# Linear attention in 64-row and 64-column groups of the array, two heads at a time

## The chip, the cores and the metric

One core of a Trainium2 chip runs the whole program as one launch. The metric is the device time of that launch in microseconds (us). TensorE (PE in the rows) multiplies, VectorE (DVE) and ScalarE (ACT) read its results from PSUM, GpSimd (POOL) works in SBUF, and SyncE issues the weight stream.

## What is computed

A trunk of two layers, 512 tokens of width 1024. Each layer mixes tokens by three groups of heads (linear attention, sparse attention, latent attention), then runs an MLP. Only the linear attention is touched, four heads with keys of 64 and values of 128, in 8 chunks of 64 tokens:

```python
q_dec = qc * jnp.exp(b)
k_inv = kc * jnp.exp(-b)
scores = jnp.where(causal, jnp.einsum('bnhcd,bnhsd->bnhcs', q_dec, k_inv), 0.0)
o_intra = jnp.einsum('bnhcs,bnhsv->bnhcv', scores, vc)
k_end = kc * jnp.exp(b_end - b)
state_inc = jnp.einsum('bnhcd,bnhcv->bnhdv', k_end, vc)
...
def step(state, inp):
    dec, inc = inp
    return dec[..., None] * state + inc, state
...
o = o_intra + jnp.einsum('bnhcd,bnhdv->bnhcv', q_dec, s_prev)
```

## The kernel before

Everything is written out by hand: one instruction stream for each engine, semaphores between them, and a table (`USES`) that gives each PSUM tile one of eight banks in a fixed order. A tile may be written once the tile before it in its bank has been read (`vacant`); `freed` says that a tile has been read, `filled` that it has been written.

A layer runs: 24 units of input projection (TensorE, matmuls of 128x128 weights on 512 columns), then the attention stage, then the output projection and the MLP.

The attention stage goes over 32 steps j (`N_ATT`), each one query block of one softmax head; the first 16 are the latent attention. For each step TensorE computes logits three steps ahead (`logits`, `LEAD`), VectorE masks them (`mask_max`), ScalarE takes exponentials, VectorE normalises (`normalise`), TensorE transposes (`turn`), ScalarE copies (`turned`), and TensorE weighs values for two steps at a time (`weigh_pair`). The linear attention is woven between these:

- `gla_scores(h)`, at the start and at j = 0, 2, 4: k_inv times q_dec, one head at a time, 128 tokens by 128 tokens. The queries lie in `gqp`, a tile of 128 rows for each head of which 64 are zero, so that the product over 128 rows holds one head only. `masked_scores` (VectorE) copies the two 64x64 diagonal blocks to `sct`, whose other blocks are zero.
- the increments, into banks `inc00` to `inc11`: `ke` holds the keys twice, each time with one of every two chunks zero. One bank holds four chunks of two heads, the heads in the column halves of the array.
- VectorE adds them up to the states `st` (lines 1474 and 1476), 7 steps for each pair of heads, each waiting for the one before.
- `gla_out(h)`, at j = 1, 3, 5, 7, one head at a time, banks 0 and 7 in turn: masked scores times values, plus states times queries.
- for each head then: square (ScalarE), `stat` (TensorE, a sum over rows by a matrix of ones), `factor` (ScalarE, logarithm and exponential), `mix` (VectorE, which also frees the bank of `gla_out`), `mix_high`, `mix_low`.

GpSimd clears `gqp`, `sct` and `ke` in each layer (lines 420, 429, 434).

A matmul in fp32 stands in the trace as two weight loads and two matmuls; "record" below means one such matmul.

Of the kernel before, what the change touches and what calls it, by code (L numbers as in the profile page):

```python
# [20 lines left out]
P = 128  # L21
# [84 lines left out]
TURNING = ["gs0"] + [f"lg{j}" for j in range(LEAD)]  # L106
for _j in range(N_MLA):
    TURNING += [f"lg{_j + LEAD}"] if _j + LEAD < N_MLA else []
    TURNING += [f"gs{SCORE_SLOT[_j]}"] if _j in SCORE_SLOT else []
    TURNING += [f"gst{STAT_SLOT[_j]}"] if _j in STAT_SLOT else []  # L110

# [10 lines left out]
def part_of(j):  # L122
# [18 lines left out]
    + [(name, (2, 3, 6)[i % 3]) for i, name in enumerate(TURNING[:1 + LEAD])]  # L141
    + [("inc00", 4), ("inc01", 5), ("inc10", 6), ("inc11", 7)]
    + [(name, (2, 3, 6)[i % 3]) for i, name in enumerate(TURNING) if i > LEAD]
# [58 lines left out]
def build_trunk(nc, x_in, stream, params, consts, out):  # L202
    with ExitStack() as ctx:
# [45 lines left out]
        sct, _ = place("sct", [P, 2, TB, P], at=a0 + 8192)  # L249
# [69 lines left out]
        zeroed = S("zeroed", 4)  # L319
# [77 lines left out]
        def _(pool):  # L397
# [18 lines left out]
            with pool.Fori(0, DEPTH) as l:  # L416

                pool.wait_ge(*x_ready.at(l, -1))
                alone(pool)
                pool.memset(gqp[:], 0.0).then_inc(zeroed.sem, 1)  # L420
                pool.wait_ge(*lo_ready.at(l, POOL_LOW[0] + AHEAD - 1))
                for u in POOL_LOW:
# [3 lines left out]
                    if u == 11:  # L426
                        pool.wait_ge(*rel_used.at(l, 3 * IDX_H - 1))
                        alone(pool)
                        pool.memset(sct[:], 0.0).then_inc(zeroed.sem, 1)
                    if u == 19:  # L430
                        pool.wait_ge(*B.filled(l, "mv1"))
                        alone(pool)
                    if u in (19, 21):
                        pool.memset(ke[:, (u - 19) // 2], 0.0).then_inc(zeroed.sem, 1)
# [22 lines left out]
        def _(pe):  # L457
# [58 lines left out]
            with pe.Fori(0, DEPTH) as l:  # L516
# [156 lines left out]
                def gla_scores(h):  # L673
                    pe.wait_ge(*B.vacant(l, f"gs{h}"))
                    for tb in range(TB):
                        tk = slice(tb * P, (tb + 1) * P)
                        m = pe.matmul(B[f"gs{h}"][:, tk], kinv[:, h // 2, tk], gqp[:, h, tk], start=True, stop=True)
                    m.then_inc(*B.on_fill(f"gs{h}"))

                def gla_out(h):  # L680
                    name = f"go{h}"
                    pe.wait_ge(*B.vacant(l, name))
                    pe.wait_ge(*B.freed(l, f"gs{h}"))
                    if h == 0:
                        pe.wait_ge(*B.freed(l, "inc11"))
                    for tb in range(TB):
                        pe.matmul(B[name][:, tb * P:(tb + 1) * P], gvt[:, tb, h * GLA_DV:(h + 1) * GLA_DV],
                                  sct[:, h % 2, tb], start=True, stop=False)
                        for c in (2 * tb, 2 * tb + 1):
                            if c == 0:  # L690
                                continue
                            m = pe.matmul(B[name][:, c * CHUNK:(c + 1) * CHUNK], st[:, c, h // 2],  # L692
                                          gqp[:, h, c * CHUNK:(c + 1) * CHUNK], start=False,
                                          stop=(c % 2 == 1))
                    m.then_inc(*B.on_fill(name))
# [67 lines left out]
                for j in range(LEAD):  # L763
                    logits(j)
# [100 lines left out]
        def _(act):  # L865
# [27 lines left out]
            with act.Fori(0, DEPTH) as l:  # L893
# [194 lines left out]
                for j in range(N_ATT):  # L1088
# [6 lines left out]
                    if j in STAT_SLOT:  # L1095
                        factor(f"gst{STAT_SLOT[j]}", GLA_DV)
# [582 lines left out]
```

## Time and profile before

| | us |
|---|---|
| median of 3 runs | 1317.99 |
| lowest and highest | 1312.17, 1323.12 |
| profiled execution | 1319.28 |
| its span | 1317.6 |
| TensorE busy | 1261.7 (96%) |
| VectorE busy | 773.5 (59%) |
| ScalarE busy | 538.5 (41%) |
| GpSimd busy | 247.3 (19%) |

The mean granted TensorE clock is 0.988 of full speed. The attention stage begins at 188.2 us in layer 0 and at 835.3 us in layer 1. "Idle before" in the rows is the time in which the engine stood still ahead of the instruction, with what ended it.

### The profile page before, as it was taken

The page shows a single profiled execution, that of the slowest core. Times are in us where ns is not written, and L with a number is a line of the kernel's source. Part 1 is how long each engine was busy: PE and PEld are TensorE (multiplying, and loading weights), DVE is VectorE, ACT ScalarE, POOL GpSimd, SP SyncE. Part 2 cuts the span into 40 slices and gives each one's busy share as a digit, 9 for nine tenths or more (in the row PEclk, how much of TensorE's full clock was granted, in tenths as well). Part 3 has the DMA queues.
Part 4 walks back from the last instruction along what each step waited for, and adds up shares of the span by engine and source line. Part 5 has one row for each costly group of instructions (what it writes and reads, how often), then busy time and mean ns, then how long its engine had stood idle before and what let it go on. Part 6 is the DMA issues. An engine that isn't in the chain of part 4 may idle for free.

```text
span 1317.6 us, 19119 instructions
## 1 busy us (share of the span) xinstructions
PE 1261.7 (96%) x5912; PEld 987.6 (75%) x5912; DVE 773.5 (59%) x1236; ACT 538.5 (41%) x863; POOL 247.3 (19%) x157
## 2 busy tenths in 40 slices
PE   4999999899999999999999999988999999999997
PEld 3856776478888888888877568765788888888886
DVE  4579866624464554544766888564445544445458
ACT  4474435734422313223436643375443132232343
POOL 4022340002021020110531323200111201102016
PEclk9999999889999999999999999999999999999999
DMA  5211220013222222222222112100232223223233
GB/s 199 99 49 64 64 97 1 2 48 122 97 98 91 101 96 96 96 96 96 96 98 81 59 54 81 65 2 1 91 113 96 96 95 100 92 96 108 89 104 127
DMA packets 31023, 110.46 MB, mean 84 GB/s; under 512 B 3568, under 2 KB 3568, under 8 KB 30960
## 3 DMA queue, kind: packets, MB, share of 16 engines
q1 hardware_dynamic: 29088, 103.82, 23.2%
q0 software_dynamic: 576, 3.76, 0.8%
q10 hardware_dynamic: 1296, 2.12, 0.5%
q8 instruction: 30, 0.49, 0.2%
q14 instruction: 33, 0.27, 0.1%
HBM read 107.59 MB, written 2.10 MB: 83 GB/s over the span
## 4 chain that ended last, share of the span: by engine, by line
PE 89%; DVE 3%; ACT 3%; issue 3%; POOL 1%; DMA 1%; DVEq 0%; ACTq 0%; SPq 0%; POOLq 0%
PE bank L821 18%; PE bank L819 18%; PE bank L820 18%; PE bank L476 6%; PE bank L477 6%; PE bank L478 6%; PE bank L510 2%; PE bank L499 2%; PE bank L498 2%; PE bank L497 2%; PE bank L708 1%; PE bank L735 1%; PE bank L720 1%; PE bank L692 1%; POOL lnb L409 1%
## 5 line engine op out<-in xcount | busy, mean ns | idle before, releaser
L874 ACT ACTIVATE wh<-raw 128x1024 fp32r<-128x1024 f32 x194 | 204.8, 1056 | 394.1 <-PE bank L821 239.0
L1153 DVE TENSOR_TENSOR wl<-raw,wh 128x1024 fp32r<-128x1024 f32 x158 | 246.9, 1563 | 98.5 <-ACT wh L874 91.0
L819 PE MATMUL bank<-hh,wl 128*128 128x512 f32 x512 | 200.0, 391 | 0.0
L819 PE MATMUL bank<-xmh,wl 128*128 128x512 f32 x512 | 199.3, 389 | 0.0
L821 PE MATMUL bank<-hl,wh 128*128 128x512 f32 x512 | 199.2, 389 | 0.0
L821 PE MATMUL bank<-xml,wh 128*128 128x512 f32 x512 | 199.2, 389 | 0.0
L820 PE MATMUL bank<-xmh,wh 128*128 128x512 f32 x512 | 199.2, 389 | 0.0
L820 PE MATMUL bank<-hh,wh 128*128 128x512 f32 x512 | 199.2, 389 | 0.0
L444 POOL TENSOR_TENSOR x<-x,rsb 128x512 f32<-128x512 f32 x64 | 84.5, 1320 | 580.3 <-DVE rsb L1531 580.3
L476 PE MATMUL bank<-xgh,wl 128*128 128x512 f32 x368 | 152.4, 414 | 22.8 <-DVE xgl L1162 17.3
L1520 DVE TENSOR_TENSOR sqb<-tf 128x512 f32<-128x512 f32 x64 | 44.3, 692 | 181.4 <-ACT hh L1124 181.4
L477 PE MATMUL bank<-xgh,wh 128*128 128x512 f32 x368 | 145.2, 394 | 0.0
L478 PE MATMUL bank<-xgl,wh 128*128 128x512 f32 x368 | 144.9, 394 | 0.0
L424 POOL TENSOR_TENSOR wl<-raw,wh 128x1024 fp32r<-128x1024 f32 x36 | 86.5, 2403 | 236.7 <-ACT wh L874 236.7
L1122 ACT ACTIVATE tf<-bank 128x512 f32<-128x512 f32 x64 | 38.3, 598 | 204.5 <-PE bank L821 204.5
L1531 DVE TENSOR_TENSOR rsb<-bank,rb 128x512 f32<-128x512 f32 x64 | 44.3, 691 | 116.8 <-PE bank L821 113.2
L820 PEld LDWEIGHTS bank<-hh,wh 128*128 128x128 f32 x512 | 96.1, 188 | 20.6 <-issue 0.5
L819 PEld LDWEIGHTS bank<-hh,wl 128*128 128x128 f32 x512 | 96.1, 188 | 20.3 <-issue 0.5
L476 PEld LDWEIGHTS bank<-xgh,wl 128*128 128x128 f32 x368 | 69.8, 190 | 55.2 <-DVE xgl L1162 21.4
L819 PEld LDWEIGHTS bank<-xmh,wl 128*128 128x128 f32 x512 | 96.1, 188 | 20.1 <-DVE xml L1162 0.4
L820 PEld LDWEIGHTS bank<-xmh,wh 128*128 128x128 f32 x512 | 96.1, 188 | 20.0
L821 PEld LDWEIGHTS bank<-xml,wh 128*128 128x128 f32 x512 | 96.1, 188 | 20.0
(187 smaller groups left out, 1757.7 us busy)
## 6 DMA issues: line engine op xcount, KB each, us to landing
raw<-in_stream SPq DMA_DIRECT2D x194, 512.0 KB, 3.2
x<-in_x ACTq DMA_DIRECT2D x8, 256.0 KB, 12.8
out_y<-x SPq DMA_DIRECT2D x8, 256.0 KB, 4.3
par<-in_params POOLq DMA_DIRECT2D x2, 916.0 KB, 4.8
con<-in_consts POOLq DMA_DIRECT2D x1, 944.5 KB, 9.1
par<-in_params POOLq DMA_DIRECT2D x1, 896.0 KB, 11.3
par<-in_params ACTq DMA_DIRECT2D x1, 20.0 KB, 2.6
```

The costliest lines, as they stand in the source:

```text
L424: pool.tensor_tensor(wl[:, u % 2], raw[:, u % 2], wh[:, u % 2], ALU.subtract)\
L444: pool.tensor_tensor(x[:, d], x[:, d], rsb[:, d % 2], ALU.add).then_inc(x_ready.sem, 1)
L476: pe.matmul(bank[:], wk_l, act_h[:, k], start=(n == 0), stop=False)
L477: pe.matmul(bank[:], wk_h, act_h[:, k], start=False, stop=False)
L478: m = pe.matmul(bank[:], wk_h, act_l[:, k], start=False, stop=last)
L819: pe.matmul(B.t[s][:], wl[:, s, n_block(k)], src_h[:, k], start=(k == 0), stop=False)
L820: pe.matmul(B.t[s][:], wh[:, s, n_block(k)], src_h[:, k], start=False, stop=False)
L821: m = pe.matmul(B.t[s][:], wh[:, s, n_block(k)], src_l[:, k], start=False, stop=(k == KB - 1))
L874: act.activation(wh[:, s], raw[:, s], ACT.Copy).then_inc(hi_ready.sem, 1)
L1153: vec.tensor_tensor(wl[:, s], raw[:, s], wh[:, s], ALU.subtract).then_inc(lo_ready.sem, 1)
L1520: vec.tensor_tensor(sqb[:, s], tf[:, s], tf[:, s], ALU.mult).then_inc(hid_ready.sem, 1)
L1531: vec.tensor_tensor(rsb[:, s], B.t[s][:], rb[:], ALU.mult).then_inc(dn_freed[s].sem, 1)
```

## The change

- Scores: 64x64 matmuls, unpadded. The rows of the array are split by head, the columns by the parity of the chunk. Both heads of a pair come from one call, `gla_scores(pr)`, each in its own bank.
- `gqp` holds both heads of a pair in one tile; `sct` holds only the diagonal blocks; `masked_scores(pr)` makes one copy of 128 rows for each head. `ke` is a plain copy.
- Increments: the rows are split by the parity of the chunk, the columns by head; banks hold even and odd chunks.
- `gla_out(pr)`: two heads into two banks, rows split in halves. Matmuls of one bank always come from one half of the rows; halfway the halves change over, and TensorE waits there for its own last matmul (`rows_done`).
- The outputs come at j = 1 and 5 (pairs), the second pair's scores at j = 2, the sums of squares at j = 3 and 7, two at a time.
- The increments are now ahead of the second and third logits, and on VectorE the second and third `mask_max` stand between the states of the first and of the second pair.
- GpSimd clears nothing.

```diff
-SCORE_SLOT = {2 * h - 2: h for h in range(1, GLA_H)}
-OUT_SLOT = {2 * h + 1: h for h in range(GLA_H)}
-STAT_SLOT = {2 * h + 3: h for h in range(GLA_H)}
+SCORE_SLOT = {2: 1}
+OUT_SLOT = {1: 0, 5: 1}
+STAT_SLOT = {3: 0, 7: 1}
...
-    + [("inc00", 4), ("inc01", 5), ("inc10", 6), ("inc11", 7)]
+    + [("inc00", 4), ("inc01", 5), ("inc10", 0), ("inc11", 1)]
...
+                def gla_scores(pr):
+                    for hp in range(2):
+                        pe.wait_ge(*B.vacant(l, f"gs{2 * pr + hp}"))
+                    alone(pe)
+                    for c in range(NCHUNK):
+                        r = slice(CHUNK * (c % 2), CHUNK * (c % 2) + CHUNK)
+                        keys = slice(c * CHUNK, (c + 1) * CHUNK)
+                        for hp in range(2):
+                            k = slice(GLA_DK * hp, GLA_DK * hp + GLA_DK)
+                            m = pe.matmul(B[f"gs{2 * pr + hp}"][r, c // 2 * CHUNK:(c // 2 + 1) * CHUNK],
+                                          kinv[k, pr, keys], gqp[k, pr, keys], start=True, stop=True)
...
+                    for c in range(0, NCHUNK, 2):
+                        within(0, c, c == 0, False)
+                        within(1, c + 1, c == 0, False)
+                        across(0, c + 1)
+                        if c > 0:
+                            across(1, c)
+                            across(0, c)
+                        mine = across(1, c + 1)
+                        if c == NCHUNK - 2:
+                            mine.then_inc(rows_done.sem, 1)
+                            pe.wait_ge(*rows_done.at(l, pr))
+                    for c in range(0, NCHUNK, 2):
+                        m0 = within(0, c + 1, False, c == NCHUNK - 2)
+                        m1 = within(1, c, False, c == NCHUNK - 2)
...
+                    for c in range(NCHUNK - 1):
+                        name = f"inc{pr}{c % 2}"
+                        r = slice(CHUNK * (c % 2), CHUNK * (c % 2) + CHUNK)
+                        for hp in range(2):
+                            h = 2 * pr + hp
+                            m = pe.matmul(B[name][hp * 64:(hp + 1) * 64, c // 2 * P:(c // 2 + 1) * P],
+                                          ke[r, 0, c // 2, h * GLA_DK:(h + 1) * GLA_DK],
+                                          gvt[r, c // 2, h * GLA_DV:(h + 1) * GLA_DV], start=True, stop=True)
...
+                masked_scores(0)
+                mask_max(0)
+                states(0)
+                for j in range(1, LEAD):
+                    mask_max(j)
+                states(1)
```

`within` is masked scores times values of one chunk (64 rows, 128 columns of the array, 64 columns moving), `across` is state times queries of one chunk, of the same shape.

TensorE at the start of the attention stage, before. The names are tiles; 128x128 after them is the output's shape, and x4 is the number of matmuls in a row.

```order
L677 MATMUL bank<-gqp,kinv 128x128 x4
L701 REGISTER_ALU
L708 MATMUL bank<-kT,qT 128x128
L701 REGISTER_ALU
L708 MATMUL bank<-kT,qT 128x128
L701 REGISTER_ALU
L708 MATMUL bank<-kT,qT 128x256
L768 REGISTER_ALU x2
L777 MATMUL bank<-gvt,ke 64x128 x14
L773 REGISTER_ALU
L777 MATMUL bank<-gvt,ke 64x128 x14
L701 REGISTER_ALU
```

The same place in the changed kernel:

```order
L662 REGISTER_ALU x2
L669 MATMUL bank<-gqp,kinv 64x64 x16
L721 MATMUL bank<-kT,qT 128x128
L779 REGISTER_ALU x2
L790 MATMUL bank<-gvt,ke 64x128 x14
L783 REGISTER_ALU x2
L790 MATMUL bank<-gvt,ke 64x128 x14
L714 REGISTER_ALU
L721 MATMUL bank<-kT,qT 128x128
L714 REGISTER_ALU
L721 MATMUL bank<-kT,qT 128x256 x2
L730 REGISTER_ALU
```

Four padded score matmuls became 16 small ones for two heads; the second and third logits moved behind the increments, whose number stays 28.

VectorE between its mask of the logits and the states, before (ISA is the masking instruction, COPY the first state of a pair):

```order
L1442 REGISTER_ALU
L1447 ISA pb,nb<-bank,con 128x128
L1447 ISA nb 128x1
L1442 REGISTER_ALU
L1447 ISA pb_92,nb<-bank,con 128x256
L1447 ISA nb 128x1
L1471 REGISTER_ALU
L1474 COPY st<-bank 128x128
L1178 REGISTER_ALU
L1476 SCALAR_TENSOR_TENSOR st<-st,e_59,bank 128x128
```

And in the changed kernel, from the last state of the first pair on:

```order
L1486 REGISTER_ALU
L1481 SCALAR_TENSOR_TENSOR st<-st,e_59,bank 128x128
L1454 REGISTER_ALU
L1459 ISA pb,nb<-bank,con 128x128
L1459 ISA nb 128x1
L1454 REGISTER_ALU
L1459 ISA pb_92,nb<-bank,con 128x256
L1459 ISA nb 128x1
L1477 REGISTER_ALU
L1479 COPY st<-bank 128x128
```

The two masks stood ahead of all states and now stand between the two pairs'.

TensorE from the sum of squares of j = 3 to the outputs of j = 5, before:

```order
L510 MATMUL bank<-sqb,ones 128x512
L701 REGISTER_ALU
L708 MATMUL bank<-kT,qT 128x512
L674 REGISTER_ALU
L677 MATMUL bank<-gqp,kinv 128x128 x4
L717 REGISTER_ALU
L718 REGISTER_ALU
L720 MATMUL bank<-con,pb 128x128 x3
L701 REGISTER_ALU
L708 MATMUL bank<-kT,qT 128x128
L718 REGISTER_ALU
L720 MATMUL bank<-con,pb 128x128 x3
```

And in the changed kernel:

```order
L497 MATMUL bank<-sqb,ones 128x512
L496 REGISTER_ALU
L497 MATMUL bank<-sqb,ones 128x512
L714 REGISTER_ALU
L721 MATMUL bank<-kT,qT 128x512
L730 REGISTER_ALU
L731 REGISTER_ALU
L733 MATMUL bank<-con,pb 128x128 x3
L721 MATMUL bank<-kT,qT 128x128
L731 REGISTER_ALU
L733 MATMUL bank<-con,pb 128x128 x3
L676 REGISTER_ALU x2
```

Two sums of squares stand where one stood, and no scores are left between them and the next outputs (behind the last row in both).

## Rows read from the trace of the kernel before

**Rows 1.** Groups by line and shape, both layers: busy us, mean ns | idle before

```profile
L692 PE MATMUL bank<-gqp,st 128*128 128x64 f32 x112 | 16.6, 267 | 0.0
...
L687 PE MATMUL bank<-sct,gvt 128*128 128x128 f32 x64 | 14.9, 316 | 1.5 <-DVE tf L1420 1.5
...
L677 PE MATMUL bank<-gqp,kinv 128*128 128x128 f32 x64 | 8.6, 278 | 2.9 <-DVE st L1476 2.9
```

**Rows 2.** Timeline of TensorE, start of the attention stage, layer 0

```profile
188.23 1.05 PE L677 MATMUL bank<-gqp,kinv 128*128 128x128 f32 x8
189.12 0.61 PE L708 MATMUL bank<-kT,qT 96*128 96x128 f32 x4
...
191.07 3.28 PE L777 MATMUL bank<-gvt,ke 128*64 128x128 f32 x56
194.28 0.70 PE L708 MATMUL bank<-kT,qT 96*128 96x256 f32 x2
196.41 1.16 PE L677 MATMUL bank<-gqp,kinv 128*128 128x128 f32 x8 [1.43 <-DVE st L1476]
198.26 0.33 PE L720 MATMUL bank<-con,pb 128*128 128x128 f32 x1 [0.69 <-DVE pb L1454]
...
199.20 0.38 PE L687 MATMUL bank<-sct,gvt 128*128 128x128 f32 x2
...
201.60 0.86 PE L708 MATMUL bank<-kT,qT 96*128 96x384 f32 x2
```

**Rows 3.** Timeline of ScalarE and then VectorE, same stretch

```profile
189.51 1.26 ACT L1057 ACTIVATE gvt<-bank,rcol 128x512 f32<-128x512 f32 x2
...
192.20 0.29 DVE L1474 COPY st<-bank 128x128 f32<-128x128 f32 x1 [0.65 <-PE bank L777]
...
197.72 0.16 DVE L1453 RECIPROCAL rinv<-rsum 128x1 f32<-128x1 f32 x1
```

**Rows 4.** Timeline of TensorE, four matmuls of the indexer in four row groups

```profile
54.28 0.31 PEld L595 LDWEIGHTS bank<-ikr,iqT 32*128 32x128 f32 x8 [0.35 <-issue]
...
54.81 0.61 PE L595 MATMUL bank<-ikr,iqT 32*128 32x512 f32 x4
...
55.35 0.50 PE L476 MATMUL bank<-xgh,wl 128*128 128x512 f32 x1
```

**Rows 5.** Timeline of TensorE, sums of squares and the last head's outputs, layer 0

```profile
207.36 1.13 PE L510 MATMUL bank<-sqb,ones 128*128 128x512 f32 x2
208.32 1.02 PE L708 MATMUL bank<-kT,qT 96*128 96x512 f32 x2
...
217.60 0.49 PE L687 MATMUL bank<-sct,gvt 128*128 128x128 f32 x2 [0.77 <-DVE tf L1420]
```

**Rows 6.** Timeline of ScalarE and VectorE after the first sum of squares

```profile
208.60 0.69 ACT L926 ACTIVATE lnb<-bank,con 128x512 f32<-128x512 f32 x1 [3.25 <-PE bank L510]
209.32 0.63 ACT L930 ACTIVATE rsb<-lnb 128x512 f32<-128x512 f32 x1
...
209.57 0.69 DVE L1447 CUSTOM_DVE_ANT_0 pb<-bank,con 128x512 f32<-128x512 f32 x1 [2.73 <-PE bank L708]
...
210.18 0.74 DVE L1420 SCALAR_TENSOR_TENSOR tf<-bank,par,rsb 128x512 f32<-128x512 f32 x1
210.96 0.69 DVE L1427 TENSOR_TENSOR tf<-tf,gg 128x512 f32<-128x512 f32 x1
```

**Rows 7.** Timeline of TensorE behind the linear attention; then busy us of PE, PEld, DVE, ACT, POOL

```profile
230.91 0.49 PE L708 MATMUL bank<-dkn,dqn 64*128 64x128 f32 x4 [1.55 <-DVE nb L1447]
...
228.00:232.00 4.00, 2.45 (x14) 1.34 (x13) 3.75 (x11) 2.88 (x9) 0.00 (x0) 0.94 0.00 0
```

**Rows 8.** A stretch of layer 1, same columns, then PEclk; then TensorE there

```profile
845.00:847.00 2.00, 1.62 (x6) 1.08 (x7) 1.53 (x9) 0.91 (x4) 0.00 (x0) 0.72 0.00 0
...
845.38 0.33 PE L720 MATMUL bank<-con,pb 128*128 128x128 f32 x1 [0.71 <-DVE pb L1454]
...
856.12 1.12 PE L510 MATMUL bank<-sqb,ones 128*128 128x512 f32 x2
```

More of the change, by code:

```diff
@@ L671, in _ @@
                 pe.wait_ge(*B.freed(l, "gk1"))
[L673 to L695, printed above, removed]
@@ new lines, in gla_out, with within, across @@
+                def gla_out(pr):
+                    for hp in range(2):
+                        pe.wait_ge(*B.vacant(l, f"go{2 * pr + hp}"))
+                        pe.wait_ge(*B.freed(l, f"gs{2 * pr + hp}"))
+                    pe.wait_ge(*B.freed(l, f"inc{pr}0"))
+                    def within(hp, c, start, last):
+                        h, r = 2 * pr + hp, slice(CHUNK * (c % 2), CHUNK * (c % 2) + CHUNK)
+                        return pe.matmul(B[f"go{h}"][:, c * CHUNK:(c + 1) * CHUNK],
+                                         gvt[r, c // 2, h * GLA_DV:(h + 1) * GLA_DV], sct[r, hp, c // 2],
+                                         start=start, stop=last)
+                    def across(hp, c):
+                        h, k = 2 * pr + hp, slice(GLA_DK * hp, GLA_DK * hp + GLA_DK)
+                        return pe.matmul(B[f"go{h}"][:, c * CHUNK:(c + 1) * CHUNK], st[k, c, pr],
+                                         gqp[k, pr, c * CHUNK:(c + 1) * CHUNK], start=False, stop=False)
+                    for c in range(0, NCHUNK, 2):
[12 more added lines that the diff above has]
+                        m1 = within(1, c, False, c == NCHUNK - 2)
+                        if c == NCHUNK - 2:
+                            m0.then_inc(*B.on_fill(f"go{2 * pr}"))
+                            m1.then_inc(*B.on_fill(f"go{2 * pr + 1}"))
@@ L762, in _ @@
                 gla_scores(0)
-                for j in range(LEAD):
-                    logits(j)
+                logits(0)
                 for tb in range(TB):
@@ L1092, in _ @@
                     if j - 1 in OUT_SLOT:
-                        h = OUT_SLOT[j - 1]
-                        square(f"gst{h}", B[f"go{h}"][:], wait=B.filled(l, f"go{h}"))
+                        for h in range(2 * OUT_SLOT[j - 1], 2 * OUT_SLOT[j - 1] + 2):
+                            square(f"gst{h}", B[f"go{h}"][:], wait=B.filled(l, f"go{h}"))
                     if j in STAT_SLOT:
-                        factor(f"gst{STAT_SLOT[j]}", GLA_DV)
+                        for h in range(2 * STAT_SLOT[j], 2 * STAT_SLOT[j] + 2):
+                            factor(f"gst{h}", GLA_DV)
                     if j - 1 in STAT_SLOT:
-                        mix_high(STAT_SLOT[j - 1], STAT_SLOT[j - 1])
+                        for h in range(2 * STAT_SLOT[j - 1], 2 * STAT_SLOT[j - 1] + 2):
+                            mix_high(h, h)
                     if j % PAIR == LAG and j > PAIR:
@@ L1496, in _ @@
                     if j - 1 in STAT_SLOT:
-                        h = STAT_SLOT[j - 1]
-                        mix(h, f"gst{h}", f"go{h}", G_GLA + h, gate=h)
+                        for h in range(2 * STAT_SLOT[j - 1], 2 * STAT_SLOT[j - 1] + 2):
+                            mix(h, f"gst{h}", f"go{h}", G_GLA + h, gate=h)
                     if j - 2 in STAT_SLOT:
-                        mix_low(STAT_SLOT[j - 2])
+                        for h in range(2 * STAT_SLOT[j - 2], 2 * STAT_SLOT[j - 2] + 2):
+                            mix_low(h)
                     if j % PAIR == LAG + 3 and j > PAIR:
```

87 lines of the change are left out of this document (32 added, 55 removed).

## The prediction

> **What bounds the kernel now.** I read the groups by line first, to see how much work the change can touch at all. The scores are 64 records over both layers, the two lines of the outputs 112 and 64 [rows 1], the increments 56 in one layer [rows 2]. In a stream they follow each other at intervals much shorter than their own durations, so their cost has to be read as start to start. Then the timeline of the attention stage of layer 0 [rows 2]: eight score records go from 188.23 to 189.12, 0.111 us each; one head's outputs go from 199.20 to 201.60, 22 records, 0.109 us each, though 14 of the 22 move only 64 columns. A record of 64 columns costs as much as one of 128 here: the load of 128 weight columns sets the pace, 0.11 us. The 56 increment records take 191.07 to 194.28, 0.057 us each, since two halves of the columns run side by side, 0.115 us for a pair.
>
> So a layer spends on TensorE: scores 4 x 0.89 = 3.56 us, increments 3.2 us, outputs 4 x 2.4 = 9.6 us, 16.4 us together, 33 us in 1317.6 [rows 1, 2]. Nothing outside can move by much, and even a halving of all of this would be 1.3%.
>
> Which engine ends a wait decides how much of it shows. From 188 to 198.3 it is VectorE: TensorE waits 1.43 and 0.69 us, and the first transpose (198.26) follows the first normalisation (197.72), which follows the chain of states from 192.2 to 197.7 [rows 2, 3]. From 198.3 to about 225 TensorE hardly waits: 0.77 us ahead of the last head's outputs, for the mix that frees its bank [rows 5]. From about 226 on VectorE takes part again: TensorE waits 1.55 us for a mask ahead of 230.91, and VectorE is busy for 3.75 of the 4 us from 228 on [rows 7].
>
> **What a record costs in row groups.** The trace of before has this for the indexer, four matmuls in four groups of 32 rows [rows 4]. Eight weight loads end within 0.31 us, where one after another they would take 8 x 0.11 = 0.9. So loads into different row groups go side by side. The second four matmuls start at 54.81, 0.53 after the first, which is a load (0.10) and 0.43 of streaming 512 columns: their own loads were done meanwhile. And the next full matmul starts at 55.35, 0.11 after the last stream's end (54.81 + 0.43), and loads again for 0.11: each change between full array and groups costs about 0.2 us in and 0.2 us out.
>
> From this, for one pair of heads, with both row halves running side by side:
> - Outputs: 30 records in each half (22 ahead of the changeover, 8 behind), each paced by its load of 128 weight columns: 30 x 0.109 = 3.27. One entry 0.2, and at the changeover the array runs dry and loads anew. No row shows a wait of TensorE for itself; from below it is a load (0.11), from above the 0.69 us of a wait for another engine [rows 2]. I take 0.35, near the low end, since no other engine works in between. The exit falls together with the entry to the next weighing. Sum 3.8 us against 2 x 2.4 = 4.8. Gain 1.0, twice in a layer.
> - Scores: each quarter of the array gets 8 records of 64 weight columns and 64 moving, half the increments' 0.109 each, 8 x 0.055 = 0.45. With entry and exit 0.85 against 1.78. Gain 0.9 for each pair.
> - Increments: 16 records for the fuller quarters at 0.109, 1.75 us against 3.2. Gain 1.45.
>
> **What of it shows**, in layer 0:
>
> Start of the stage. The increments start when ScalarE has copied the values (189.51 + 1.26 = 190.8, [rows 3]), which nothing changes. The first pair's 28 records now take 8 x 0.109 + 0.1, and the state chain needs all of them where it needed 16 records before (0.92 us): it starts at 192.2 again. It is as long as it was, 14 steps, but with two masks in between, 0.2 and 0.4 us. So the first transpose is 0.6 us later, at about 198.85. What scores and increments save here becomes TensorE's idle time: it would be done at 194.2 and stand for 4.6 us. Cost +0.6.
>
> Outputs of both pairs: -2.0. The second pair's scores, at j = 2: -0.9.
>
> The second pair's outputs, at j = 5. They wait for the banks of both heads of the first pair, freed by two mixes on VectorE. Before, head 2 at j = 5 needed one mix only, and started right when it was done (210.18 + 0.74, [rows 6]). Now the two sums of squares take 2 x 0.96 us [rows 5], the factor of the second head another 1.3 us of ScalarE behind the first (0.69 + 0.63), and the second mix stands behind a whole first (0.74 + 0.69). Counted from TensorE's own order: sums of squares start about 207.1 and end 209.0; logits of 512 columns to 209.9; transposes and logits to 210.8. On the other side: these logits are read at 210.1 and masked to 210.75, first mix to 212.1, second mix frees the bank at 212.85. TensorE stands for 2.1 us. Before, it stood 0.77 us at j = 7, which goes. Cost +1.3.
>
> Sum to the last sum of squares: 0.6 - 2.0 - 0.9 + 1.3 = -1.0. Behind that VectorE decides [rows 7]. The same operations stand there in another order (the mix of head 3 comes earlier, together with that of head 2); their start comes about 0.5 us earlier as I count it, since two factors must now end before the second mix. I keep -0.5 of the -1.0.
>
> Off the path, at nothing: GpSimd's clears (GpSimd is 81% idle), one multiplication of 0.69 us for each pair on VectorE in the projection, where TensorE is fully busy, and two of four copies of `ke` on ScalarE, which waits for TensorE next to them. If their cover went, they could only shorten the time.
>
> Layer 1 has the same shape. Both: -1.0 us.
>
> **The clock.** The granted clock drops to its lower level (1.2 GHz, 0.5 of full) now and then in the attention stage. One place is telling: in layer 1 it is 0.72 on average from 845 to 847, right after TensorE had stood 0.71 us [rows 8]; in layer 0, after nearly the same waits, it stayed up. From its first transpose (845.38) to the first sum of squares (856.12) it takes 10.74 us, layer 0, at full clock, 198.26 to 207.36, 9.10 [rows 2, 5]. A drop there costs 1.64 us. The change gives TensorE a longer rest just there, 4.6 us, so I expect the drop in both layers: +1.6.
>
> The sum on the profiled execution: 1319.28 - 1.0 + 1.6 = 1319.9, and the median of the runs lies 1.3 below the profiled one: **1318.6, say 1319 us.** The three runs spread from 1312 to 1323, so 1% (13 us) is about what a measurement can tell.
>
> **Rivals.**
>
> *TensorE is all that counts.* If the waits I added (2 x 0.6 and 2 x 1.3) don't come, and the work behind moves up with it, then -2.9 in a layer remains of the window, and with a changeover near 0.1 us -3.4: 6 to 7 us, some 1311 without the extra drop of the clock. Against it speak two chains I can write down step by step. 0.15.
>
> *Weight loads aren't hidden in the small groups (slower).* If loads of the two halves go one after another, the outputs of a pair take 60 x 0.11 = 6.6 + 0.55 = 7.1 instead of 4.8: +2.3 twice in a layer, while the scores (64 columns a load, 32 x 0.055 = 1.8 + 0.4) lose 0.4 instead of gaining 0.9. A layer then comes to 4.6 + 0.4 + 1.9 (the two waits) = +6.9 at the most, some 14 us, 1333 with the clock's part. It decides from 0.14 us a record: at 30 x 0.14 + 0.55 the outputs of a pair cost 4.8, as now. The eight loads in 0.31 us speak against it [rows 4], but they are one burst and not a stream. A milder form: the halves run side by side, but in each half load and stream add up, 0.11 + 0.055 = 0.165 a record. Then a pair's outputs take 30 x 0.165 + 0.55 = 5.5, +0.7 twice, a pair's scores 8 x 0.11 + 0.4 = 1.3, -0.5, and with the two waits (+1.9) a layer comes to +2.8: 5.6 and the clock's 1.6 make 1325. 0.07 for both, 0.04 of it the milder.
> The Trainium skill's page "TensorE: Matmul & The Clock Gate" says, in Part 3 under "What overlaps and what doesn't", that a weight load overlaps matmuls in flight only where the row group differs, which is the milder form. This trace disagrees: four of the eight loads were done while matmuls of the same four row groups ran, since the second matmuls follow the first without one.
>
> *The clock (slower).* The rests of 4.6 and 2.1 us bring a second drop in each layer, at 1.6 each: 1319 + 3.3 = 1322, or with a longer first drop 1326. For it: the drop shown here followed a wait. Against: a later drop of the stage could as well go when the work in front of it moves. 0.16.
>
> *The main case*, the waits eat the gain: 0.62: 1319.
>
> **Range.** The unknown costs (changeover 0.1 to 0.7, four times: -1 to +1.4; a drop more or less: 1.6 each) give 1314 to 1324 for the main case. With the median's own scatter and the clock's case up to 1326 I give 1311 to 1327. Faster than 1305 would need more than all of TensorE's savings on the path: 0.03. Slower than 1331 needs the weight loads one after another (0.03) or several long drops of the clock (0.01): 0.04. The rest, 0.93, is no change that can be told.
>
> **What the profile would show.** Right: the first transpose of each layer about 0.6 us later after the stage's start, TensorE idle over 4 us ahead of it; a pair's outputs in about 3.8 us, starts in both row halves side by side; a wait of about 2 us for the mix (the changed kernel's L1432) ahead of the second pair's outputs; clock 0.5 after the first rest in both layers. Wrong: outputs of a pair over 4.8 us, or no wait at j = 5; a longer stretch at half clock through the small matmuls would make the whole prediction wrong.

## The result, and the profile after

| | before | changed |
|---|---|---|
| median of 6 runs each, us | 1318.6 | 1336.55 |
| lowest and highest | 1312.17, 1323.12 | 1334.9, 1339.89 |
| profiled execution, its span | 1319.28, 1317.6 | 1339.89, 1338.2 |
| mean granted TensorE clock | 0.988 | 0.968 |

The ratio is 1.0147 with a 95% interval of 1.012 to 1.0173: slower by 1.5%, outside the forecast range of 1311 to 1327.

The six changed runs had granted clocks of 0.968 to 0.976; the profiled execution is the longest of them, so half-clock times read from it are above those of the median run.

TensorE's timeline at the start of the attention stage of layer 0, changed kernel; it answers to [rows 2, 3, 5, 6].

```profile
187.88 0.69 PE L669 MATMUL bank<-gqp,kinv 64*64 64x64 f32 x32
188.50 0.49 PE L721 MATMUL bank<-kT,qT 96*128 96x128 f32 x2
190.60 1.96 PE L790 MATMUL bank<-gvt,ke 64*64 64x128 f32 x56 [1.61 <-ACT gvt L1071]
192.49 1.35 PE L721 MATMUL bank<-kT,qT 96*128 96x128 f32 x6
198.61 0.47 PE L733 MATMUL bank<-con,pb 128*128 128x128 f32 x1 [4.76 <-DVE pb L1466]
...
200.50 0.69 PE L682 MATMUL bank<-sct,gvt 64*128 64x64 f32 x4
...
205.53 1.97 PE L682 MATMUL bank<-sct,gvt 64*128 64x64 f32 x16
207.44 1.65 PE L721 MATMUL bank<-kT,qT 96*128 96x384 f32 x2
...
213.93 3.52 PE L497 MATMUL bank<-sqb,ones 128*128 128x512 f32 x4 [0.41 <-DVE sct L1427]
...
221.33 0.44 PE L682 MATMUL bank<-sct,gvt 64*128 64x64 f32 x4 [2.15 <-DVE tf L1432]
...
224.07 1.97 PE L682 MATMUL bank<-sct,gvt 64*128 64x64 f32 x16
225.97 1.12 PE L748 MATMUL bank<-pt,vm 128*64 128x128 f32 x8
```

Read as a list of starts, the forecast looks good: scores of a pair in 0.62 us, increments in 1.89, the first transpose 10.73 us after the stage's start (before 10.03), a rest of 4.76 us ahead of it, a wait of 2.15 us for the mix at 221.33. What isn't as forecast is the pace. The first pair's outputs take 200.50 to 207.44, 6.9 us for work counted at 3.8, and the first sum of squares comes 26.05 us after the stage's start, where it came at 19.13 [rows 5]. The windows of the same stretches say why (columns: length, busy time and count of each engine, granted clock, DMA share, GB/s). Before:

```profile
196.00:206.00 10.00, 8.90 (x64) 7.60 (x65) 7.20 (x26) 3.49 (x11) 0.00 (x0) 1.00 0.00 0
206.00:217.00 11.00, 10.83 (x78) 8.47 (x77) 6.31 (x20) 6.27 (x14) 0.00 (x0) 1.00 0.01 2
```

Changed:

```profile
196.00:206.00 10.00, 7.32 (x52) 6.08 (x54) 4.33 (x18) 1.79 (x6) 0.00 (x0) 0.53 0.00 1
206.00:217.00 11.00, 10.60 (x64) 5.85 (x63) 2.92 (x10) 3.21 (x8) 0.00 (x0) 0.50 0.01 1
...
237.00:247.00 10.00, 8.01 (x26) 3.65 (x27) 7.25 (x24) 5.44 (x15) 0.00 (x0) 0.70 0.00 0
```

The granted clock is at its lower level (0.5, 1.2 GHz) from 196.6 on for 20.5 us, which is 2.8 us into the rest of 4.76; in layer 1 it is from 848.5 on for as long. That is not behind the long rest, which comes 4.9 us later there, but 0.6 us into the increments, which had waited 1.61 us for ScalarE's values:

```profile
847.88 3.09 PE L790 MATMUL bank<-gvt,ke 64*64 64x128 f32 x56 [1.61 <-ACT gvt L1071]
856.43 0.48 PE L733 MATMUL bank<-con,pb 128*128 128x128 f32 x1 [3.04 <-DVE pb L1466]
```

Over the whole execution the records have 89.0 us at 0.5, before 33.4. An attention stage (its start to the first MLP matmul) is 138.81 and 136.86 us long, before 128.76 and 126.12: +20.8, all that separates the two profiled executions (20.6; the medians differ by 18). 55.5 us more at half the rate cost at most 27.8.

How far the changed kernel is behind the one before at the transposes of step j, both counted from the stage's start (us):

| | j = 0 | 3 | 5 | 7 | 9 | 11 | 15 |
|---|---|---|---|---|---|---|---|
| layer 0 | 0.7 | 8.3 | 8.4 | 13.4 | 11.5 | 13.1 | 12.9 |
| layer 1 | 1.2 | 6.7 | 5.2 | 10.5 | 8.3 | 9.9 | 9.8 |

By its place in the order the changed kernel has made one head's outputs more than the kernel before at j = 3 and 7, and one sum of squares more (0.96 us) at j = 5 and 9; at j = 11 both are level. The first stretch at half clock makes the step up to j = 5. From j = 5 to 9, with the wait of 2.15 us for the mix in between, 3.1 us are lost in each layer. A drop follows that rest too, 6.8 us from 223.9 on and from 879.3 on in layer 1, where the kernel before has none:

```profile
224.00:231.00 7.00, 6.93 (x47) 5.87 (x48) 2.39 (x12) 2.34 (x8) 0.00 (x0) 0.52 0.01 2
```

There is one more place, late in the stage. TensorE and VectorE of the changed kernel, from the second pair's sums of squares on; it answers to [rows 7]:

```profile
238.15 0.44 PE L733 MATMUL bank<-con,pb 128*128 128x128 f32 x2 [1.69 <-DVE pb L1466]
238.42 1.02 PE L721 MATMUL bank<-kT,qT 96*128 96x512 f32 x2
240.29 0.44 PE L733 MATMUL bank<-con,pb 128*128 128x128 f32 x2 [0.84 <-DVE pb L1466]
```

```profile
234.76 0.75 DVE L1432 SCALAR_TENSOR_TENSOR tf<-bank,par,rsb 128x512 f32<-128x512 f32 x1
235.55 0.69 DVE L1439 TENSOR_TENSOR tf<-tf,gg 128x512 f32<-128x512 f32 x1
236.16 0.74 DVE L1432 SCALAR_TENSOR_TENSOR tf<-bank,par,rsb 128x512 f32<-128x512 f32 x1
236.94 0.69 DVE L1439 TENSOR_TENSOR tf<-tf,gg 128x512 f32<-128x512 f32 x1
237.55 0.15 DVE L1465 RECIPROCAL rinv<-rsum 128x1 f32<-128x1 f32 x1
237.74 0.35 DVE L1466 TENSOR_SCALAR pb<-pb,rinv 128x256 f32<-128x256 f32 x1
...
238.48 1.29 DVE L1445 TENSOR_TENSOR xgl<-tf,xgh 128x512 fp32r<-128x512 f32 x2
```

Two mixes stand in a row, and the normalisation that TensorE needs (237.74) stands behind both; the next stands behind two subtractions. From j = 9 to 11 this adds 1.6 us in each layer, 2.5 with the sum of squares that only the kernel before has between them. Nothing more is lost up to j = 15, although the clock drops here as well (6.8 us from 241.0 on): the kernel before has a wait of 1.55 us and a drop of 3.4 us at the same place (from 231.5 on). So of the 22.7 us that both layers have lost by j = 15, about 12 come by j = 5, 6 around the second pair's outputs, and 5 here.

### The profile page after: what moved, and what is told of

It reads as the page before. It is cut to its first block, busy times and chain, and to the rows that moved or that the text cites. A ratio compares the mean times of both kernels' runs of the same rounds, so it can differ in the third digit from the quotient of the medians.

```text
span 1338.2 us, 19293 instructions
## 1 busy us (share of the span) xinstructions
PE 1273.2 (95%) x6040; PEld 988.9 (74%) x6040; DVE 766.8 (57%) x1224; ACT 537.0 (40%) x859; POOL 238.7 (18%) x149
## 4 chain that ended last, share of the span: by engine, by line
PE 89%; DVE 3%; issue 3%; ACT 3%; POOL 1%; DMA 1%; DVEq 0%; ACTq 0%; SPq 0%; POOLq 0%
PE bank L836 17%; PE bank L835 17%; PE bank L837 17%; PE bank L463 6%; PE bank L464 6%; PE bank L465 6%; PE bank L497 3%; PE bank L721 2%; PE bank L485 2%; PE bank L486 2%; PE bank L484 2%; PE bank L733 1%; PE bank L748 1%; PE bank L682 1%; POOL lnb L408 1%
## 5 line engine op out<-in xcount | busy, mean ns | idle before, releaser
L463 PE MATMUL bank<-xgh,wl 128*128 128x512 f32 x368 | 153.0, 416 | 22.7 <-DVE xgl L1178 17.0
L1533 DVE TENSOR_TENSOR sqb<-tf 128x512 f32<-128x512 f32 x64 | 44.3, 693 | 181.3 <-ACT hh L1140 181.3
L835 PEld LDWEIGHTS bank<-hh,wl 128*128 128x128 f32 x512 | 96.1, 188 | 20.5 <-issue 0.5
L835 PEld LDWEIGHTS bank<-xmh,wl 128*128 128x128 f32 x512 | 96.1, 188 | 20.5 <-DVE xml L1178 0.4
L1544 DVE TENSOR_TENSOR rsb<-bank,rb 128x512 f32<-128x512 f32 x64 | 44.3, 692 | 116.7 <-PE bank L837 113.0
L837 PEld LDWEIGHTS bank<-hl,wh 128*128 128x128 f32 x512 | 96.1, 188 | 19.9
## 6 DMA issues: line engine op xcount, KB each, us to landing
par<-in_params POOLq DMA_DIRECT2D x1, 896.0 KB, 11.3
```

The costliest lines, as they stand in the source:

```text
L463: pe.matmul(bank[:], wk_l, act_h[:, k], start=(n == 0), stop=False)
L835: pe.matmul(B.t[s][:], wl[:, s, n_block(k)], src_h[:, k], start=(k == 0), stop=False)
L837: m = pe.matmul(B.t[s][:], wh[:, s, n_block(k)], src_l[:, k], start=False, stop=(k == KB - 1))
L1533: vec.tensor_tensor(sqb[:, s], tf[:, s], tf[:, s], ALU.mult).then_inc(hid_ready.sem, 1)
L1544: vec.tensor_tensor(rsb[:, s], B.t[s][:], rb[:], ALU.mult).then_inc(dn_freed[s].sem, 1)
```

## The experiments

In each the ratio is to the kernel before on the same chip; "half clock" is the time at 0.5 in the profiled execution (before 33.4). Ratios count the runs, half clock is one execution; so the granted clock of the median run stands beside it (before 0.991 or 0.992 on each of these chips; the changed kernel 0.973). Four theories: **A** (in two forecasts called R), a longer rest drops the clock; **B**, small matmuls hold it down; **C**, the new order's waits alone; **D**, the outputs of two heads in a row hold it down.

| run | us | ratio, 95% interval | half clock | clock, median |
|---|---|---|---|---|
| s_pad | 1349.81 | 1.0258 [1.0207, 1.0308] | 81.3 | 0.9725 |
| s_out | 1342.76 | 1.0206 [1.0173, 1.024] | 68.0 | 0.9745 |
| s_scinc | 1342.4 | 1.0191 [1.0156, 1.0226] | 70.9 | 0.9735 |
| warm4 | 1329.19 | 1.0087 [1.0058, 1.0117] | 61.7 | 0.9805 |
| f_front | 1324.28 | 1.0075 [1.0042, 1.0108] | 33.1 | 0.986 |
| f_pairout | 1324.64 | 1.0081 [1.0048, 1.0113] | 54.6 | 0.988 |
| g_before | 1323.53 | 1.0061 [1.0037, 1.0085] | 47.4 | 0.9845 |
| g_warm | 1318.17 | 1.0032 [1.0011, 1.0053] | 30.9 | 0.9895 |
| b_delay | 1326.99 | 1.0105 [1.0067, 1.0144] | 40.8 | 0.9865 |
| a_dense | 1336.19 | 1.0147 [1.0112, 1.0182] | 58.2 | 0.980 |
| a_late | 1334.89 | 1.0146 [1.0113, 1.018] | 71.8 | 0.975 |
| g_late | 1310.9 | 0.9964 [0.9943, 0.9986] | 23.8 | 0.9915 |
| b_states | 1310.5 | 0.9954 [0.9937, 0.997] | 23.9 | 0.993 |
| a_states | 1328.07 | 1.0083 [1.0052, 1.0114] | 44.3 | 0.976 |

### The groups by themselves: s_pad, s_out, s_scinc

The changed kernel with all tiles padded as before, its order kept (s_pad); the same with the outputs in row halves (s_out), or with scores and increments in quarters (s_scinc). The edit of s_pad in the outputs:

```diff
-                        within(0, c, c == 0, False)
-                        within(1, c + 1, c == 0, False)
...
+                            pe.matmul(B[name][:, tb * P:(tb + 1) * P], gvt[:, tb, h * GLA_DV:(h + 1) * GLA_DV],
+                                      sct[:, hp, tb], start=True, stop=False)
```

> The changed kernel's order, pairs and slots, but all its matmuls padded over the full array as before (the two padded tiles and the clears are back). Theory A (the longer rest of TensorE ahead of the first transpose drops the clock, which then stays down): the rest shrinks from 4.8 to about 3.3 us, since scores and increments take 1.8 and 3.2 us again; a drop of the clock remains, 1325 to 1335 us. Theory B (matmuls in halves and quarters of the array hold the clock down, whatever the rests): no long drop, 1316 to 1323 us. Theory C (the order alone costs it, by its waits): the wait of 2 us ahead of the second pair's outputs is there and the time is near the changed kernel's 1336 us at a clock near the old one.

> As the run of the padded kernel in the new order, with one part put back: the outputs in 64-row halves (scores and increments padded). Theory A: as that run, within 3 us, since the rest is the same. Theory B: the clock stays down through the outputs; 8 to 14 us more than the padded run, half-clock stretches of 10 us or more after the outputs' start.

> The padded kernel in the new order, with scores and increments in quarters of the array, outputs padded. The rest ahead of the first transpose is 4.7 us as in the changed kernel. Theory A: clock down for about 20 us after it in both layers, 1333 to 1340 us. Theory B, if only the outputs hold it down: one drop of 3.4 or 6.8 us, at most 1326 us.

B is refuted: with the matmul shapes of the kernel before, the time is 13 us longer. A's forecast for s_pad (1325 to 1335) was too low as well, and s_out is 7 us below s_pad, where A had within 3 us and B 8 to 14 more; s_scinc lies where A had it (1342.4). The groups save 7.1 us (outputs) and 7.4 us (scores and increments), and both together 13.3 (1349.8 to 1336.55). So the loss is the order's: s_pad is 2.6% above before with the same matmuls. Its 47.9 us more at half clock cost at most 23.9 of the 32.6 us between the profiled executions; at least 8.7 us, by that estimate, are the order's waits and work at any clock, which is C's part. The outputs of a pair in s_pad, layer 0, at half clock:

```profile
201.43 0.64 PE L690 MATMUL bank<-sct,gvt 128*128 128x128 f32 x2
...
210.71 1.59 PE L711 MATMUL bank<-kT,qT 96*128 96x384 f32 x2
```

44 records in 9.28 us, 0.211 each, twice the 0.109 of [rows 2]: the pace of these load-paced records goes with the clock too. In row halves the same work took 6.9 us.

### The two parts of the order: f_front, f_pairout

The kernel before, padded, with only the changed front (both heads' scores first, increments ahead of two logits, masks between the states), or with only the outputs, squares, factors and mixes in pairs:

```diff
-OUT_SLOT = {2 * h + 1: h for h in range(GLA_H)}
-STAT_SLOT = {2 * h + 3: h for h in range(GLA_H)}
+OUT_SLOT = {1: 0, 5: 1}
+STAT_SLOT = {3: 0, 7: 1}
```

> The kernel before with the changed kernel's front only: both heads' scores first, increments ahead of the second and third logits, the masks between the states. Everything padded; outputs one head at a time at j = 1, 3, 5, 7 as before. Theory R (the longer rest of TensorE ahead of the first transpose drops the clock and that costs it): the clock is down for 13 us or so after the rest, 1330 us or more. Theory D (what holds the clock down is the outputs of two heads in a row, over 9 us of matmuls that each wait for a load of 128 weight columns and move 64 columns): one short drop at most, below 1325 us.

> The kernel before with the pairing only: outputs of two heads in a row at j = 1 and 5, their sums of squares at j = 3 and 7, everything padded, the front as before. Theory D: drops of 10 us or more that begin in or before the outputs, 1335 us or more. Theory R: rest as before, 1.4 and 0.7 us; below 1325 us.

f_front costs 9.2 and f_pairout 9.6 us. Both are below 1325 us, so the front alone went against theory R (1330 or more), and the pairs alone against D (1335 or more). s_pad, which has both, costs some 32. But it has more than both: the second pair's scores come together, and the increments lie in banks by parity, so that its first transpose is 1.59 us later than before (f_front: 0.83). What makes up the 13 us between 32 and the sum of the two isn't separated. f_front has a rest of 3.46 us; its profiled execution has no more half clock in all than before, but that is one of its two shortest, and the runs' clock (0.986 against 0.992) says that most of the 9.2 us is clock (0.6% of 1324 is 8). f_pairout keeps the short rest (0.70 us), and its profiled execution (1331.23) is the longest of its runs. It shows the two waits by themselves:

```profile
229.83 0.44 PE L720 MATMUL bank<-con,pb 128*128 128x128 f32 x2 [1.70 <-DVE pb L1457]
230.10 1.02 PE L708 MATMUL bank<-kT,qT 96*128 96x512 f32 x2
232.05 0.44 PE L720 MATMUL bank<-con,pb 128*128 128x128 f32 x2 [0.93 <-DVE pb L1457]
```

Half clock follows there for 6.8 us from 232.5. Another 10.2 us from 263.2 stand behind a wait for a mask (1.72 us) that the kernel before has too, with a drop as long in layer 0 (from 258.8).

### The rest ahead of the first transpose: b_delay, g_before, g_warm, warm4

b_delay puts eight VectorE copies ahead of the first normalisation of the kernel before. g_before is the kernel before with scores and increments in groups, one head at a time; g_warm adds three full matmuls in the rest, warm4 four of them to the changed kernel. Nobody reads their result.

```diff
+                for i in range(8):
+                    link(vec.tensor_copy(mpad[:, i % 2], con[:, C_SCAN:C_SCAN + T]))
                 normalise(0)
```

```diff
+                for i in range(4):
+                    pe.matmul(B.t[7][:], gvt[:, i % TB, 0:P], gvt[:, i % TB], start=True, stop=True)
                 for j in range(N_ATT + LAG):
```

> The kernel before with eight VectorE copies in a chain ahead of the first normalisation; TensorE's rest ahead of the first transpose grows from 0.7 us to about 5 us in each layer, nothing else changes. Only the time of the delay: 2 x 4.2 = +8.5 us, ratio 1.0065, half-clock time as before (33 us). Rest alone gives the long drop (theory A): half clock for about 20 us after the rest in both layers, +8.5 + 17, ratio 1.019, half-clock time 65 to 70 us. Rest and two heads' outputs in a row are both needed for the long one (where I stand): one short drop more in a layer at most, half-clock time 37 to 47 us, ratio 1.008 to 1.011.

> The kernel before in its own order, scores in quarters of the array one head at a time, increments in quarters (banks by parity), outputs padded and one head at a time. TensorE gets through its front earlier and rests for about 3.5 us in one piece ahead of the first transpose. Theory R: a long drop there, 1325 us or more. Theory D: 1314 to 1320 us with a drop of 3.4 or 6.8 us at most.

> As the run of the groups in the old order, with three extra full-array matmuls of 512 columns (values nobody reads) in the rest ahead of the first transpose. If the rest is what drops the clock there: no drop between the start of the stage and the last sum of squares, 1310 to 1316 us. If the outputs drop it also one head at a time: a drop remains in the first 20 us behind the rest, and the time is that of the run without extra matmuls.

> The changed kernel with four extra full-array matmuls of 512 columns (values nobody reads) in the rest ahead of the first transpose, some 3.9 us of its 4.8. Theory A: no drop there, full clock through the first pair's outputs, 1318 to 1324 us. Theory B: the clock still falls during the first pair's outputs and stays down for over 10 us, 1330 us or more.

The first transpose of b_delay, and the windows over its rest (197.46 to 201.84) and behind it:

```profile
201.84 0.48 PE L720 MATMUL bank<-con,pb 128*128 128x128 f32 x1 [4.38 <-DVE pb L1454]
```

```profile
196.00:206.00 10.00, 5.31 (x24) 4.41 (x25) 8.18 (x26) 1.84 (x6) 0.00 (x0) 0.58 0.00 0
206.00:217.00 11.00, 11.00 (x58) 8.91 (x58) 3.10 (x10) 2.05 (x6) 0.00 (x0) 0.76 0.00 1
```

A longer rest alone costs clock, in the old order and with padded matmuls (0.9865 against 0.992 in the runs). Where the drop begins is not settled by it: in layer 0 it is on record from 197.6, 0.1 us after the rest began and 4.2 us before its end, so the rest can have drawn it out but hardly started it. b_delay adds 2 x 3.7 us of rest and costs 11.3. That is more than the delay itself (2 x 3.7 = 7.4, ratio 1.0056, below the interval), though with no more half clock than I expected (40.8). Filling the rest of g_before gives back 5.4 us (half clock 47.4 to 30.9), filling that of the changed kernel 7.4 us (1336.55 to 1329.19). Both came out above what the rest theory had (1310 to 1316, and 1318 to 1324), and g_before itself (1323.5) between theory R (1325 or more) and D (1314 to 1320). warm4's profiled execution, the longest of its six, still drops in layer 0, in the middle of the first pair's outputs (from 200.7 on, 10.2 us). In layer 1 its drop is on record from 845.8 on, in the increments, and over before the first transpose; behind that the whole first pair runs at full clock, 9.08 us from the first transpose to the first sum of squares:

```profile
854.99 0.27 PE L733 MATMUL bank<-con,pb 128*128 128x128 f32 x1
...
864.07 1.96 PE L497 MATMUL bank<-sqb,ones 128*128 128x512 f32 x4 [0.87 <-DVE sct L1429]
```

All runs side by side, the rest ahead of the first transpose against the half-clock stretch that begins in it or behind it, ahead of the first sum of squares (layer 0 / layer 1). A stretch can begin inside the rest, and that part of it costs nothing:

| run | rest, us | stretch, us |
|---|---|---|
| b_states | 0 / 0 | none / none |
| before | 0.69 / 0.71 | none / 3.4 |
| f_pairout | 0.70 / 0.70 | 3.4 / 3.4 |
| g_late | 1.19 / 1.20 | none / none |
| warm4 (changed order) | 1.32 / 0 | 10.2 / none (6.8 ahead) |
| a_dense (changed order) | 1.32 / 0 | none / none (6.8 ahead) |
| g_warm | 1.41 / 1.42 | 3.4 / none |
| a_states | 1.94 / 1.95 | 3.4 / 3.4 |
| g_before | 3.04 / 4.00 | 13.7 (3.4 ahead) / 6.8 |
| f_front | 3.46 / 3.47 | 6.8 / 3.4 |
| s_pad, s_out (changed order) | 4.11 / 4.12 | 13.7 / 13.7 |
| b_delay | 4.38 / 4.40 | 13.7 / 6.8 |
| s_scinc (changed order) | 4.76 / 3.47 | 17.1 / 17.1 (3.4 ahead) |
| a_late (changed order) | 4.76 / 4.76 | 13.7 / 17.1 |
| changed | 4.76 / 3.04 | 20.5 / 20.5 (begins 4.9 ahead of the rest) |

The longer the rest, the longer the stretch, with a large scatter; the changed order has the longest. "Ahead" marks drops that begin in the increments: four in layer 1, all behind the wait of 1.61 or 1.75 us that the new order puts there, and one in layer 0 of g_before, behind a wait of 0.48 us.

### What else could hold the clock: a_dense, a_late

a_dense is warm4 with three full matmuls in and around the first pair's outputs. a_late is the changed kernel with the second pair's sums of squares one at a time:

```diff
-STAT_SLOT = {3: 0, 7: 1}
+STAT_SLOT = {3: (0, 1), 7: (2,), 9: (3,)}
```

> The kernel with the filled rest (four full matmuls) and, in the first pair's outputs, three more full matmuls of 512 columns whose result nobody reads: ahead of the outputs, at the changeover, behind them. Theory D (outputs of two heads in a row are sparse work that keeps the clock down): the first drop ends after 3.4 us in place of 10.2 and 6.8; half-clock time falls from 62 to 48 us, and that pays the 2 x 2.6 us of filler in part: ratio 1.007. Against D: half-clock time stays at 60 or more, the filler adds 5 to 8 us to the run with the filled rest: ratio 1.013 to 1.015.

> The changed kernel, with the sums of squares of the second pair one at a time again (j = 7 and 9, as in the kernel before, with factor, mix and halves behind them). If the two mixes in a row are the cause of TensorE's waits of 1.7 and 0.9 us ahead of the tenth and eleventh transposes: both go, -5 us over two layers, and the drops that follow them get shorter: ratio 1.006 to 1.009. If these waits come from VectorE's whole load there: they move behind the ninth step, ratio 1.013 to 1.016.

a_dense lacks the one drop at the first pair that warm4 had, in layer 0, and has the same two as warm4 in layer 1 (6.8 and 10.2 us), where neither is at the first pair; in all 58.2 us, and a ratio of 1.0147 against 1.0087, near what I had expected if D is wrong (60 or more, 1.013 to 1.015). D isn't shown by it, and warm4's layer 1, where the same outputs ran at full clock, speaks against D alone. In a_late both waits (1.69, 0.84) go, so the mixes in a row were their cause. One for a mask stands there instead, as it did before [rows 7]:

```profile
239.87 0.80 PE L721 MATMUL bank<-dkn,dqn 64*128 64x128 f32 x4 [1.79 <-DVE nb L1459]
```

The stage gets 3.1 and 2.0 us shorter in the profiles, but the ratio is 1.0146 against 1.0147, no difference, where I had expected 1.006 to 1.009. So the mixes in a row cause the two waits, and taking them away gains nothing that can be told.

### Taking the rest away by moving work: g_late, b_states, a_states

The second pair's states aren't needed until that pair's outputs. In g_late (g_before), b_states (the kernel before, padded) and a_states (the changed kernel) they stand in three pieces behind the first three normalisations, the increments of that pair in banks 1 and 7:

```diff
+LATE = {0: (0, 1, 2), 1: (3, 4), 2: (5, 6)}
...
+                    if j in LATE:
+                        states(1, LATE[j])
```

a_states must also move the outputs to j = 3 and 7, since a pair of outputs takes bank 7, and with them the second pair's scores and the sums of squares; it isn't a test of the states alone.

> The kernel before with scores and increments unpadded in groups, one head at a time, and the states of the second pair no longer ahead of the first normalisation, but in three pieces behind the first three. If the state chain ahead of the first transpose is what the front costs: the first transpose 2.7 us earlier in both layers, TensorE's rest gone, no drop there: 5 to 8 us below before, ratio 0.994 to 0.996. Rival: VectorE becomes the bound in j = 0 to 3 and TensorE waits there instead: ratio 1.000 to 1.004.

> The kernel before, everything padded, with only the second pair's states moved behind the first three normalisations (its increments in banks 1 and 7). If the shorter state chain alone makes the gain of the run with groups and late states: half-clock time 24 to 30 us, ratio 0.996 to 0.998. If the groups are needed for it (the padded increments and scores then stand on TensorE's path, 1.2 + 0.2 us and more in a layer): ratio 0.999 to 1.001.

> The changed kernel with the second pair's states moved in the same way; since its banks 0 and 7 are taken by the outputs of a pair, the outputs move to j = 3 and 7, the scores of the second pair to j = 4, the sums of squares to j = 5 and 9. Rest ahead of the first transpose about 1.2 us in place of 4.8. If that rest is the root of the loss: 3.4 us off the front in each layer, half-clock time from 89 to 40 to 50 us, ratio 0.998 to 1.002. If the outputs of two heads in a row hold the clock down by themselves (theory D): half-clock time stays above 60 us, ratio 1.005 to 1.010.

The front of b_states: no wait ahead of the first transpose, which comes 7.48 us after the stage's start instead of 10.03.

```profile
190.60 3.28 PE L778 MATMUL bank<-gvt,ke 128*64 128x128 f32 x56
193.81 0.70 PE L709 MATMUL bank<-kT,qT 96*128 96x256 f32 x2
194.34 1.06 PE L678 MATMUL bank<-gqp,kinv 128*128 128x128 f32 x8
195.24 0.27 PE L721 MATMUL bank<-con,pb 128*128 128x128 f32 x1
```

Both padded and grouped are faster than the kernel before, b_states by 0.46% and g_late by 0.36%, intervals below 1 (though less than 1%). g_late does its increments and scores in less time, and then TensorE rests 1.19 us ahead of the same transpose (7.25 us after the start): in this order the groups gain nothing that can be told. a_states, with pairs and row halves, has a new wait of 0.67 us for states, and one of 2.06 us for the mix (changed kernel 2.15, before 0.77):

```profile
195.75 0.33 PE L734 MATMUL bank<-con,pb 128*128 128x128 f32 x1 [1.94 <-DVE pb L1467]
201.16 0.44 PE L683 MATMUL bank<-sct,gvt 64*128 64x64 f32 x4 [0.67 <-DVE st L1482]
214.46 0.44 PE L683 MATMUL bank<-sct,gvt 64*128 64x64 f32 x4 [2.06 <-DVE tf L1433]
```

Its six runs spread from 1318.7 to 1331.5, and the clock with them (0.984 for the shortest two, 0.974 to 0.977 for the rest); the profile is of the shortest, so its 44 us of half clock understate the median run, which by its clock of 0.976 has some 64 (an estimate: 2 x 0.024 of its time). So neither forecast, the rest's nor D's, fits all of its runs. It gives back 8.5 us of the 18, not all: both kernels with outputs in pairs and a short rest (a_states, f_pairout) stay 0.8% above before.

## Why the prediction was wrong

**Right, step by step.** The front: first transpose +0.70 us in layer 0 (+0.6 counted; +1.22 in layer 1, where the increments ran at half clock), rest 4.76 (4.6). Wait for the mix 2.15 (2.1). Increments 1.89 (1.75), scores 0.62 (0.85 with both changeovers). Outputs of a pair in row halves: 2.74 us from 221.33 to 224.07 for the 22 records of each half ahead of the changeover, nearly all at full clock, and 1.90 for the 8 behind it at half clock. Halving that gives some 3.7 in all, 3.8 counted. The milder form of the load rival wanted 22 x 0.165 = 3.6 ahead of the changeover alone.
The Trainium skill's page "TensorE: Matmul & The Clock Gate" (Part 3, "What overlaps and what doesn't") has a weight load overlap matmuls only where the row group differs, which is that form; these 2.74 us disagree as [rows 4] did.

**First failed step: the clock, a term mis-sized.** "A drop there costs 1.64 us ... so I expect the drop in both layers: +1.6." The drop came in both layers, in layer 0 where I said and, as far as the experiments tell, for the reason I gave; in layer 1 it began ahead of the long rest, behind the 1.61 us that TensorE waits for the values, a rest that the prediction didn't count at all. The size was read from one row, a drop that followed 0.71 us of rest [rows 8], and carried over to a rest of 4.6. It was 20.5 us long in each layer, and from the first transpose to the first sum of squares TensorE took 15.32 and 14.76 us, where before it took 9.10 and 10.74. At full clock the changed order passes there in 9.08 us (warm4, layer 1). So the term counted at +1.6 was 6.2 + 5.7 - 1.6 = 10.3 us.
The rival on the clock ("The rests of 4.6 and 2.1 us bring a second drop in each layer") was right in sign and place: 6.8 us at half clock stand behind the second rest in each layer too, at most 3.4 us of cost each. Its price, 1.6 a drop, was too low in the same way, and "several long drops of the clock" were given 0.01. b_delay shows what a test in the kernel before would have said: 13.60 and 10.93 us for the same stretch, 4.7 more than before in both layers together. That is nearer, and still less than half of the 10.3.

**Second failed step: "Behind that VectorE decides ... I keep -0.5."** I counted the mixes at their first place (j = 5) and not again behind the last sums of squares, where two mixes and two subtractions now stand in a row ahead of normalisations that TensorE waits for: 1.69 + 0.84 us, 2.5 in each layer. f_pairout has the waits alone, a_late takes them away, and its ratio doesn't move; this step weighs less than the clock.

**A third, of less weight: "Outputs of both pairs: -2.0. The second pair's scores, at j = 2: -0.9."** These savings were real on TensorE (13.3 us over both layers in the changed order, against 5.8 counted; how much of that is work which stood at half clock isn't separated), but in the order of before nothing of the scores' and increments' part is left (g_late against b_states). For outputs in row halves this wasn't tried: they need the pair.

Shown: a longer rest costs clock and a filled one gives some back (b_delay, g_warm, warm4), and the loss is the order's (s_pad). Open: why s_pad costs 32 us where its front and its pairs alone cost 9 to 10 each, and what makes the stretch 20.5 us long in the changed kernel and 13.7 and 6.8 in b_delay at nearly the same rest. Outputs of two heads in a row as a second condition beside a rest would fit the table of rests (13.7 us and more in all of the changed order with over 3 us of rest, 3.4 to 13.7 in the old order); a_dense doesn't support it, and no run takes the pairs alone out of the changed kernel. No run takes the wait ahead of the increments, or that for the mix, out of the changed kernel.

## What to carry over

A rest of TensorE costs more than its length: at rests of 4 us and more this kernel ran 7 to 20 us at half rate. So price a change that lengthens one by a delay put into the old kernel (here it would have given 4.7 us for a term taken as 1.6, still too little), and remove the rest by moving the work it waits for (the states not yet needed: 0.46%, 6 to 7 us, the best version here) rather than by making TensorE's share of it shorter. Look at every rest that the new order makes, also the short ones. Don't read one profiled execution's clock as the kernel's: where the runs scatter, take the granted clock of all of them. And where two heads' steps are joined, follow each joined step to its last use: on every engine the second one stands ahead of whatever was queued behind the first.

## Of the hardware, not expected

The clock's lower level held for anything from 3.4 to 20.5 us at a rest, and came at rests as short as 0.7 us (f_pairout, both layers) while others of 1.2 us passed without it (g_late, both layers). It stayed down while TensorE was busy nearly without a gap: in the changed kernel's window from 206 to 217 us 10.60 of 11 us busy, clock 0.50. At half clock records paced by their weight loads took 0.211 us, at full clock 0.109.
